# Reading the late projections' weights twice: blocks 3 and 4 in block 2's merge

## The reference

```python
h = rms_norm(x, lp['g_mix_pre']) * (1.0 + sc_a) + sh_a
proj = h @ lp['w_in']
z, xbc, dt_raw, q, k, v, o, gate_raw, merge_raw = jnp.split(proj, ...)
...                      # two scans, forward and backward: y (SSD), hm (mLSTM)
y_ssd = rms_norm(y * silu(z), ...) @ lp['w_ssd_out']
y_ml = (rms_norm(hm, ...) * sigmoid(o)) @ lp['w_mlstm_out']
mixed = (gate_ssd * y_ssd + gate_ml * y_ml) @ lp['w_out']
x1 = x + gt_a * rms_norm(mixed, lp['g_mix_post'])
h2 = rms_norm(x1, lp['g_ffn_pre']) * (1.0 + sc_f) + sh_f
f = peer_ffn(h2, ...)
x2 = x1 + gt_f * rms_norm(f, lp['g_ffn_post'])
```

## Time and profile before

| what | value |
|---|---|
| median of 3 runs | 2779.46 us (2779.38 to 2780.43) |
| profiled execution, span from first to last instruction | 2775.8 us |
| profiled execution, time around the span | not recorded; the median of the runs is 3.7 us above the span |
| TensorE busy | 2437.5 us (88%) |
| VectorE busy | 1590.1 us (57%) |
| ScalarE busy | 899.7 us (32%) |
| GpSimd busy | 800.3 us (29%) |
| moved by DMA | 945.78 MB, 341 GB/s over the span |
| gathers of experts | 640 |

### The profile page before, as it was taken

The page is one execution under the profiler, slowest core; times in us unless marked ns, Lnnn a source line. Parts: engine busy times, 40 slices in busy tenths (PEclk is TensorE's granted clock), DMA queues, the critical chain, the costliest instruction groups (busy, mean ns, idle before and its releaser), DMA issues.

```text
span 2775.8 us, 26857 instructions
## 1 busy us (share of the span) xinstructions
PE 2437.5 (88%) x8530; PEld 1359.7 (49%) x8530; DVE 1590.1 (57%) x3736; ACT 899.7 (32%) x2386; POOL 800.3 (29%) x705
## 2 busy tenths in 40 slices
PE   6999999978999778799889899898898988887786
PEld 3555554355888543455444465443554444343332
DVE  2320022211478776788656798556787557666674
ACT  3100121021123332454423554334544324343332
POOL 0111100000123122343333343334343334444452
PEclk9999999988999889899999999999999999999999
DMA  6222315865799789999999999999999999999996
GB/s 258 99 99 99 114 54 218 331 245 214 279 352 376 291 329 426 407 409 383 426 426 426 423 385 407 427 426 426 411 372 424 426 426 410 422 426 427 427 424 282
DMA packets 144576, 945.78 MB, mean 341 GB/s; under 512 B 17026, under 2 KB 28546, under 8 KB 40370
## 3 DMA queue, kind: packets, MB, share of 16 engines
q0 software_dynamic: 96928, 687.39, 60.0%
q1 hardware_dynamic: 34274, 208.44, 19.1%
q10 hardware_dynamic: 13232, 48.24, 4.4%
HBM read 908.82 MB, written 35.19 MB: 340 GB/s over the span
## 4 chain that ended last, share of the span: by engine, by line
PE 32%; DMA 26%; DVE 10%; ACT 4%; issue 2%; DVEq 2%; POOL 1%; ACTq 1%; POOLq 0%
DMA ring<-in_peer_uv,e_idx 25%; PE e_acc L1766 15%; PE e_acc L1695 5%; DVE ring L1898 4%; PE e_qs L1781 3%; PE e_B L1677 2%; DMA e_wb<-in_w_out 2%; PE e_A L1677 1%; ACT e_diag L1625 1%; POOL ring L1509 1%; DVEq L1900 1%; DVE e_f L1914 1%; ACT e_coef L1618 1%; PE e_A L943 0%; ACT e_mg L1003 0%
## 5 line engine op out<-in xcount | busy, mean ns | idle before, releaser
L1766 PE MATMUL e_acc<-ring,e_diag 128*128 128x512 f32 x2368 | 1122.8, 621 | 213.5 <-ACT e_diag L1625 213.3
L1509 POOL DMA_INDIRECT ring<-in_peer_uv,e_idx x640 | 760.3, 1188 | 1426.8 <-PE e_acc L1766 1024.3
L1898 DVE CUSTOM_DVE_ANT_0 ring<-ring,e_xb 128x1024 f32<-128x1024 f32 x640 | 775.1, 1224 | 437.5 <-DMA ring<-in_peer_uv,e_idx 416.5
L1766 PEld LDWEIGHTS e_acc<-ring,e_diag 128*128 128x128 f32 x2368 | 450.3, 197 | 800.2 <-issue 481.8
L1615 ACT ACTIVATE e_act<-e_dots 128x2 f32<-128x2 f32 x320 | 65.1, 204 | 754.0 <-DVEq L1900 751.6
L534 PE MATMUL pj<-held,ring 128*128 128x512 f32 x512 | 225.2, 593 | 0.0
L1625 ACT ACTIVATE e_diag<-ident,e_coef 128x128 f32<-128x128 f32 x592 | 206.1, 394 | 21.5 <-issue 0.7
L568 PE MATMUL pj<-ring,held 128*128 128x512 f32 x352 | 158.9, 607 | 11.3 <-DMA ring<-in_w_big 9.1
L1618 ACT ACTIVATE e_coef<-e_act,e_gate 128x1 f32<-128x1 f32 x640 | 153.8, 287 | 22.8 <-issue 0.7
L1781 PEld LDWEIGHTS e_qs<-e_h2T,e_w_head 128*128 128x128 f32 x1280 | 150.7, 195 | 10.8 <-issue 10.4
L1781 PE MATMUL e_qs<-e_h2T,e_w_head 128*128 128x128 f32 x1280 | 152.1, 278 | 0.8 <-ACT e_h2T L1594 0.8
(11 more groups left out here) (397 smaller groups left out, 2284.6 us busy)
## 6 DMA issues: line engine op xcount, KB each, us to landing
e_wb<-in_w_out SPq DMA_DIRECT2D x60, 1024.0 KB, 8.9
e_w_head<-in_w_q ACTq DMA_DIRECT2D x39, 1024.0 KB, 8.8
ring<-in_w_big SPq DMA_DIRECT2D x18, 2048.0 KB, 8.8
ring<-in_w_mod SPq DMA_DIRECT2D x8, 2048.0 KB, 12.2
ring<-in_peer_uv,e_idx POOLq DMA_INDIRECT x640, 13.1
wm<-in_w_mod SPq DMA_DIRECT2D x4, 2048.0 KB, 18.1
e_m<-scratch_mod_rows SPq DMA_DIRECT2D x15, 512.0 KB, 15.7
e_m<-scratch_xbcT SPq DMA_DIRECT2D x7, 1024.0 KB, 13.6
```

What stands on the lines that cost most here:

```text
L1509: nc.gpsimd.indirect_dma_start(expert[:, u % RING, :], None, dr["peer_uv"], bass.IndirectOffsetOnAxis(idx[:, h % 4, s:s + 1], 0)).then_inc ...
L1766: mm = nc.tensor.matmul(acc[:, c * 512:(c + 1) * 512], diag[:, v % RING, :], expert[:, v % RING, D + c * 512:D + (c + 1) * 512], start=Fal ...
L1898: nc.vector.tensor_tensor_reduce(expert[:, u % RING, 0:D], expert[:, u % RING, 0:D], xb[p % 2][:, :], 1.0, 0.0, ALU.mult, ALU.add, dots[:, ...
```

## The change

1. A late unit is now one weight tile for blocks 1 and 2 alone: 14 units instead of 28, each with its own load. Units 0 to 4 stay in block 0's merge; the loads of units 2, 3 and 4 go to ring slots 5, 3 and 2, and are issued at step 22 of that merge. Units 5 to 13 run at the steps 2, 4, ..., 18 of the first window.
2. Blocks 3 and 4 get their late projections as 14 `far` units in block 2's window (`KEPT_BLOCK` = 2) at the steps 31, 33, ..., 57. Each reads its weight tile again, into `far_w` (one own tile and the scans' key region of `held`). TensorE writes to `bankS`, ScalarE copies and stores one step later.
3. ScalarE keeps `hT` of blocks 3 and 4 in an own tile, `hT_kept`, by one copy at step 20 of the first window.
4. 28 products more go to VectorE: every second expert from number 160 to 215 (heads 10 to 13). Block 1's sum is closed by VectorE too (`vector_sum`).
5. The load of block 3's keys moves from step 30 of block 2's window to step 0 of block 3's. `S2` and `cand2` become views of `hot`. The memory for GpSimd's DMA descriptors is set to 4096 bytes instead of the default. The gathers wait for five late units at their start, instead of six at the fifth gather.

```diff
-LATE_UNITS, LATE_FIRST = 2 * len(LATE), 4
+LATE_UNITS, LATE_FIRST, LATE_EARLY = len(LATE), 4, 5
+LATE_STEPS = {2 * (u - LATE_EARLY) + 2: u for u in range(LATE_EARLY, LATE_UNITS)}
+LATE_RESULT_STEP = 2 * (LATE_UNITS - LATE_EARLY) + 2
+KEPT_BLOCK, FAR_FROM = 2, 31
+FAR_STEPS = {FAR_FROM + 2 * v: v for v in range(LATE_UNITS)}
-ON_VECTOR = [u < 2 * TOPK or u < 6 * TOPK and u % 4 == 0 for u in range(HEADS * TOPK)]
+ON_VECTOR = [u < 2 * TOPK or u < 6 * TOPK and u % 4 == 0 or 160 <= u < 216 and u % 2 == 0 for u in range(HEADS * TOPK)]
+VECTOR_FIRST = (0, 160)
+VECTOR_BLOCKS = (0, 1)
...
+        S2, cand2 = hot[:, 0, :, :].rearrange("p (a k) j -> p a (k j)", a=2), hot[:, 1, :, :]
+        hT_kept, far_own = sb("hT_kept", [P, KT, 2 * P]), sb("far_w", [P, KT, 2 * P])
...
-            units = [at // 2 + 4] if at < 15 and at >= 2 and at % 2 == 0 else [at - 3] if 15 <= at < LATE_UNITS + 3 else []
+            units = [LATE_STEPS[at]] if at in LATE_STEPS else []
...
+                if p == KEPT_BLOCK and x - 1 in FAR_STEPS:
+                    far(FAR_STEPS[x - 1], True)
+                if p == KEPT_BLOCK and x in FAR_STEPS:
+                    far(FAR_STEPS[x], False)
...
             def scan(j, s):
+                if j == KEPT_BLOCK and s == 0:
+                    sp.wait_ge(far_mm, LATE_UNITS)
+                    load_qk(j)
...
-                elif u >= 8 and u % 2 == 0 and i + 1 < len(LATE):
+                elif u > LATE_EARLY and u + 1 < LATE_UNITS:
                     sp.wait_ge(late_mm, u)
-                    late_load(i + 1)
+                    late_load(u + 1)
+            def far_load(v):
+                sp.dma_start(far_w[v % 2][:, :, :], dr["w_late"][v]).then_inc(far_in[v % 2], 16)
+            def far(v, result):
+                if not result and 0 < v < LATE_UNITS - 1:
+                    sp.wait_ge(far_mm, v)
+                    far_load(v + 1)
...
+                    if p == 0:
+                        for u in range(2, LATE_EARLY):
+                            late_load(u)
...
         def _(pool):
+            pool.wait_ge(late_mm, LATE_EARLY)
...
-                    pool.wait_ge(late_mm, LATE_FIRST + 2)
...
+            def far(v, result):                      # ScalarE
+                if not result:
+                    return
+                if v >= 2:
+                    act.wait_ge(late_out[v % 2], late_stored + 16 * (v // 2))
+                act.wait_ge(far_mm, v + 1)
+                nc.scalar.copy(far_from[v % 2], bankS[:, :])
+                act.drain()
+                act.sem_inc(far_free, 1)
+                act.dma_start(dr["proj"].rearrange("b p n -> p b n")[:, 3:5, 256 * LATE[v]:256 * (LATE[v] + 1)],
+                              far_from[v % 2].rearrange("p (b n) -> p b n", n=256)).then_inc(late_out[v % 2], 16)
...
+            def far(v, result):                      # TensorE
+                if result:
+                    return
+                pe.wait_ge(far_in[v % 2], 16 * (v // 2) + 16)
+                if v:
+                    pe.wait_ge(far_free, v)
+                else:
+                    pe.wait_ge(kept, 1)
+                    pe.wait_ge(chunk_done, KEPT_BLOCK)
+                for b in range(2):
+                    for k in range(KT):
+                        last = nc.tensor.matmul(bankS[:, 256 * b:256 * (b + 1)], hT_kept[:, k, b * P:(b + 1) * P], far_w[v % 2][:, k, :],
+                                                start=(k == 0), stop=(k == KT - 1))
+                last.then_inc(far_mm, 1)
...
-            def first_sum():
-                dve.wait_ge(f_mm, 1)
+            def vector_sum(p):
+                dve.wait_ge(f_mm, p + 1)
...
-    nc = bacc.Bacc("TRN2", target_bir_lowering=False, num_devices=1)
+    nc = bacc.Bacc("TRN2", target_bir_lowering=False, num_devices=1, dynamic_dma_scratch_size=4096)
```

More of the change, by code:

```diff
@@ L1331, in experts @@
         pieces_of = lambda ap: ap.rearrange("p (k n) -> p k n", n=256)
-        late_w = [pieces_of(expert[:, i, :]) for i in (6, 7, 5)]
-        late_w += [(mg[:, :, :].rearrange("p q (k n) -> p (q k) n", n=256), pieces_of(m23[:, :]))[i % 2] for i in range(3, len(LATE))]
+        late_w = [pieces_of(expert[:, i, :]) for i in (6, 7, 5, 3, 2)]
+        late_w += [(mg[:, :, :].rearrange("p q (k n) -> p (q k) n", n=256), pieces_of(m23[:, :]))[i % 2] for i in range(LATE_EARLY, LATE_UNITS)]
         late_to = [acc[:, 0:512], acc[:, 512:1024], bankS[:, :], qs[:, :]]
@@ L1349, in window_one, with interleave @@
             return units, [BACK_LIST[i] for i in backs], steps
-        def interleave(late, back, scan, merge, prepare, body, finish, body_first=False):
+        def interleave(late, back, scan, merge, far, prepare, body, finish, body_first=False):
             def at_step(p, x):
@@ L1437, in merge @@
                             sp.wait_ge(late_out[j], 16 * LATE_UNITS // 2)
+                    elif p == KEPT_BLOCK + 1:
+                        for j in range(2):
+                            sp.wait_ge(late_out[j], 2 * late_stored)
                     if not p:
@@ L1467, in merge @@
                     load_x(p)
-                elif x == 30 and p and p + 1 < BLOCKS:
+                elif x == 30 and p and p + 1 < BLOCKS and p != KEPT_BLOCK:
                     load_qk(p)
@@ L1494, in _ @@
             sp.dma_start(keys[:, :, :], dr["keysT"]).then_inc(keys_in, 16)
-            interleave(late, back, scan, merge, prepare, body, finish)
+            interleave(late, back, scan, merge, far, prepare, body, finish)
         @block.gpsimd
         def _(pool):
+            pool.wait_ge(late_mm, LATE_EARLY)
             for u in range(HEADS * TOPK):
@@ L1596, in block_sum @@
             def block_sum(p):
-                if p:
+                if p not in VECTOR_BLOCKS:
                     act.wait_ge(f_mm, p + 1)
@@ L1654, in body @@
                     run(m, n)
-                if c * GROUPS + n == LATE_UNITS + 2:
+                if c * GROUPS + n == LATE_RESULT_STEP:
                     late_result(LATE_UNITS - 1)
+                    nc.scalar.copy(hT_kept[:, :, :], hT[:, :, 3 * P:TOK]).then_inc(kept, 1)
             def finish():
@@ L1680, in scan @@
             def scan(j, s):
+                if j == KEPT_BLOCK and s == 0:
+                    pe.wait_ge(far_free, LATE_UNITS)
                 pe_scan(j, s, (lambda: pe.wait_ge(h2_ready, j + 1)) if j else (lambda: pe.wait_ge(backs_done, CHUNKS - 1)))
@@ L1686, in late @@
             def late(u):
-                i, pair = u // 2, u % 2
-                if pair == 0:
-                    pe.wait_ge(late_in[i % 2], 16 * (i // 2) + 16)
+                pe.wait_ge(late_in[late_signal[u]], late_landed[u])
                 if u >= LATE_FIRST:
@@ L1692, in late @@
                 for b in range(2):
-                    tokens = slice((1 + 2 * pair + b) * P, (2 + 2 * pair + b) * P)
+                    tokens = slice((1 + b) * P, (2 + b) * P)
                     for k in range(KT):
-                        last = nc.tensor.matmul(late_to[u][:, 256 * b:256 * (b + 1)], hT[:, k, tokens], late_w[i][:, k, :],
+                        last = nc.tensor.matmul(late_to[u][:, 256 * b:256 * (b + 1)], hT[:, k, tokens], late_w[u][:, k, :],
                                                 start=(k == 0), stop=(k == KT - 1))
                 last.then_inc(late_mm, 1)
+            def far(v, result):
[12 more added lines that the diff above has]
+                last.then_inc(far_mm, 1)
             def merge(p, x):
@@ L1821, in late, with far @@
             def late(u):
+                pass
+            def far(v, result):
                 pass
@@ L1885, in merge @@
                     dve.wait_ge(shift_in, 16 * p + 16)
+                    if p == KEPT_BLOCK:
+                        for parity in range(2):
+                            dve.wait_ge(late_out[parity], 2 * late_stored)
                     nc.vector.tensor_tensor(xb[p % 2][:, :], T[1][:, :], T[7][:, :], ALU.add).then_inc(h2_ready, 1)
@@ L2005, in body @@
                     vector_products(m - (n == 0), (n - 1) % GROUPS)
-                if m == HP and n == 0:
-                    first_sum()
+                if m and m % HP == 0 and n == 0 and m // HP - 1 in VECTOR_BLOCKS:
+                    vector_sum(m // HP - 1)
                 if m and m % HP == 0:
@@ L2027, in _ @@
             nc.vector.memset(zero[:, :], 0.0).then_inc(const_ready, 1)
-            interleave(late, back, scan, merge, prepare, body, finish, body_first=True)
+            interleave(late, back, scan, merge, far, prepare, body, finish, body_first=True)
 def programme(nc, dr):
```

35 lines of the change are left out of this document (20 added, 15 removed).

## The result

The changed kernel takes 2821.9 us (median of 4 runs, 2814.84 to 2827.47) against 2779.94 of the kernel before in the same session: ratio 1.0151, 95% interval 1.0130 to 1.0171. It is slower, by 42 us. The forecast was 2814.5, with 2784 to 2840 as its range.

The account below looks back on a forecast made before the run. TensorE was taken to bound the first window, with VectorE close behind in its heads, and full DMA block 2's far stretch. -14 + 48 + 1 = +35 us on the profiled span, its rest unchanged, gave 2814.5 us, range 2784 to 2840.

Parts of the forecast that it names:

- the first window's 14 us of gain: First window: 12 + 6 us gained by fewer late units, 4 us lost to late weights; bounds 0 and 35.7.
- The bytes of block 2's window, 43.1 us: Block 2's window: 18.35 MB of added weight loads and stores at 426 GB/s cannot hide; 43.1 us, the lower end.
- TensorE's need, 52 us, near the bytes: Block 2's window: net 48.6 us more TensorE work, with diagonal waits kept at 18.6 us, needs 52 us more.
- The value of 48: Block 2's window: cost taken as 48 us, between 43 by bytes and 52 by TensorE.
- By the LDWEIGHTS share TensorE had half its time free: Block 2's window: skill's reading, 77.7 of 172 us, so bytes alone cost 43 us; the forecast did not follow it.
- What the late units gain in the first window, 12 + 6 us: First window: 12 us from two units fewer before L929's matmuls, 6 us from the other 12 units leaving later.
- The late weights, 4 us, bounds 0 and 12: First window: SyncE's new order and one load per unit make weights land late; 4 us lost, bounds 0 and 12.
- The first rival: First window bound by TensorE to its end, giving back all 96.7 us: 2736 us, chance 0.10.
- The second: Rival: first window gains 35.7 us, block 2's window pays bytes alone, some in lulls: about 0, 2779 us, chance 0.06.
- The third: Rival: block 2's far weights land late, from 16 us landing; at 18.4, +28 us, 2842 us, chance 0.12.
- Descriptor memory at 0: GpSimd's gathers: the ring cut to 4096 bytes costs 0, since at most 8 gathers are under way.
- What would show it: Signs if right: heads 0 and 1 about 135 us, far steps 215 to 224 us, DMA at least 420 GB/s.

Follow-up runs that it names:

- the last two experiments: Mixes reading only the last 3 or 5 weight tiles twice, four late-weight buffers, 14 more VectorE products, against the kernel before: 2777.79 and 2781.14 us.

## Why the prediction was right, and where it was not

The call, slower by 35 us with a range of 2784 to 2840, holds against 42. Part of that closeness is luck: the sum was made for the profiled execution, and there it is 13.3 us short (35 against 48.3), nearly all of it in one term, the first window's 14 us of gain that came out as 0.5. Step by step:

- **The bytes of block 2's window, 43.1 us.** Right: with all bytes and 84.7 us less TensorE work, its window is 437.9 us, 46.4 over before.
- **TensorE's need, 52 us, near the bytes.** Right in kind, too dear by some 10: with 12.6 MB taken away the window still pays 41.0. What I had kept at 18.6 us, the waits for diagonals, is 11.3 there. In the changed kernel it shrank to 6.1, and 9.6 us of waits for far weights came beside it. The value of 48 was met by 48.8, VectorE's sum (1 us) within. TensorE's waits from 1350 to 1575:

```profile
PE e_spare L1757 <- DMA e_far_w<-in_w_late: 9.6, 2, 7.1
PE e_acc L1828 <- ACT e_diag L1671: 6.1, 5, 3.1
```

- **By the LDWEIGHTS share TensorE had half its time free.** The measurement decides against the Trainium skill's rule here ("Perfetto Trace Analysis", section "Identifying the Most-Contended Engine"), as far as the share of LDWEIGHTS goes; the share of peak arithmetic, which the section names beside it, was not worked out. In the kernel without the 28 products the LDWEIGHTS share is 161.9 of 250 us, 65%, and TensorE is busy 247.9 and sets the pace: 48.1 us of work more cost 24.8 us.
- **What the late units gain in the first window, 12 + 6 us.** Right in their sum: with the weights there in time, the first window is 17.9 us shorter than before. The split was off: L933 comes 85.1 us after the window's start (675.6) instead of 100.2, 15.1 us sooner, and 2.8 come behind it. VectorE is its bound then, as 12 products less on it show (12.3 us more).
- **The late weights, 4 us, bounds 0 and 12.** This is the term that was mis-sized. TensorE's waits for them were 11.0 us, inside the bounds, but the change from two buffers to four returned 17.4 us in the first window (480.1 to 462.8; 12 to 17 against the five kernels with two buffers), so their price lies at or over the upper bound. I had costed the landing at 9.8 us from a median; the load for unit 12 took 17.7. That the store of 1 MB just ahead of it in SyncE's queue made it slow is read from the traces (17.7 and 17.4 us right behind that store, 10.5 us when issued 8.6 us behind it), and no run has the store alone moved. The lateness fell exactly on the unit in front of the matmul that VectorE waits for, so VectorE's wait there was 16.0 us, where with timely weights it was 5.2. The unit in the one place with a gain was the one that waited longest for its weights.
- **The first rival** (all 96.7 us given back) is out: with timely weights the window gives 17.9. **The second** needed 35.7 us there: out. **The third**, late far weights, is there in part: they landed in 13.5 to 13.8 us at the median, under the 16 from which it decides, and two of 14 units waited.
- **Descriptor memory at 0.** Right, by the kernel that has that alone.
- **What would show it.** Heads 0 and 1 (744.4 to 897 before) took 145.8 us, from 749.8 to 895.6, not 135; VectorE was over 85% busy only behind the late unit. TensorE's idle from 675.4 to 744.0, put at 4 us, was 4.7, with 3.2 of it for late weights and xbcT, so the sign set at 5 us was just not reached. The far steps took some 223 us, from the first far matmul at 1351.4 to the last at 1574.2, within 215 to 224, with DMA at 417 GB/s over that stretch instead of 420 or more. Blocks 3 and 4 kept their length within 3 us. So the signs of heads 0 and 1 did not come, and those of block 2's window came in the main.

The median rose less (42 us) than the span of the profiled execution (48.3): the four runs of the changed kernel spread over 12.6 us. That is no mark of the change: beside the last two experiments the kernel before spread from 2776.07 to 2789.69 us in 23 runs. Where the spread comes from stays open.

## What to carry to other kernels

Before work is moved off a full engine, look for the second engine behind it, place by place: here 96.7 us of TensorE work were worth 17.9 at best, 15.1 of it in front of one matmul, while their second reading cost its full bytes where DMA was full. When each unit gets its own load, cost the landing of the load for the unit that matters, with what stands before it in its queue at that moment, and not by the median of the run. The first few units moved are worth most: 3 of 14 tiles won 10.3 us for 8.1, the next two won 1.3 for 6.9 (the 1.3 is less than one profile can tell, but the medians agree: 3.4 us between the two kernels).

## What the runs showed of the hardware

With its late units gone, TensorE was busy 43.6 of 117.7 us between 777.9 and 895.6 and its granted clock was 0.61 there, down from 0.97 in the earlier trace rows: for the most part the lower of its two levels, 1.2 GHz. The same four matmuls of 257 columns that took 1.03 us in the earlier trace rows took 2.08 in this stage of the changed kernel, behind an idle time of 4 to 20 us:

```profile
794.67 2.08 PE L984 MATMUL e_A<-e_wb,e_m 128*128 128x257 f32 x4 [9.49 <-DVEq L1157]
...
801.88 2.08 PE L984 MATMUL e_A<-e_wb,e_m 128*128 128x257 f32 x4 [4.28 <-DVE e_wb L1215]
...
870.81 2.08 PE L984 MATMUL e_A<-e_wb,e_m 128*128 128x257 f32 x4 [20.19 <-DVEq L1157]
```

It cost little here, since VectorE set the pace and waited 1.3 us in all for these matmuls (L984).
